# Seven block products in place of eight in the up projections of two feed-forward layers, with the modulation moved to the down projections

## The reference

```python
FFN_HIDDEN = 2816                               # 22 chunks of 128

def swiglu_ffn(x, w_in, w_down):
    h = x @ w_in                                # [512, 1024] @ [1024, 5632]
    g, u = h[..., :FFN_HIDDEN], h[..., FFN_HIDDEN:]
    return (jax.nn.silu(g) * u) @ w_down        # [512, 2816] @ [2816, 1024]

# layers 0 and 1
y = swiglu_ffn(x, ffn_w_in[i], ffn_w_down[i])
x = layer_norm(ALPHA * x + y, ln_g[i, 2], ln_b[i, 2])

# third block
c_act = jax.nn.silu(c)                                  # [1, 1024]
mod = (c_act @ mod_w[l] + mod_b[l])[:, None, :]         # [1024, 6144]: 48 blocks of 128 columns
```

## Time and profile before

| | |
|---|---|
| runs | 2298.22, 2318.23, 2323.58 us, median 2318.23 |
| profiled execution | span 2302.4 us, 47528 instructions |
| PE | busy 2235.3 us, 97% |
| DVE | busy 1271.0 us, 55% |
| ACT | busy 936.0 us, 41% |
| POOL | busy 298.9 us, 13% |
| granted clock of PE, mean | 0.994 |

### The profile page before, as it was taken

The page is one execution under the profiler, slowest core; times in us unless marked ns, Lnnn a source line. Parts: engine busy times, 40 slices in busy tenths (PEclk is TensorE's granted clock), DMA queues, the critical chain, the costliest instruction groups (busy, mean ns, idle before and its releaser), DMA issues.

```text
span 2302.4 us, 47528 instructions
## 1 busy us (share of the span) xinstructions
PE 2235.3 (97%) x18842; PEld 2140.7 (93%) x18846; DVE 1271.0 (55%) x2590; ACT 936.0 (41%) x1547; POOL 298.9 (13%) x318
## 2 busy tenths in 40 slices
PE   7999999999999999989999999999999998999998
PEld 7978999999999996978999999999989898999998
DVE  6477443665553256889463476554165655656513
ACT  4566354332222143478363252222144554444312
POOL 3000300200000052336120110000033002000001
PEclk9999999999999999999999999999999999999999
DMA  6333341255542221200252245553312202333221
GB/s 172 81 94 92 104 143 56 83 140 142 138 137 101 91 66 56 74 2 1 92 164 75 74 110 140 154 144 110 106 49 92 79 20 75 91 104 97 95 106 55
DMA packets 303947, 219.07 MB, mean 95 GB/s; under 512 B 34442, under 2 KB 290384, under 8 KB 303824
## 3 DMA queue, kind: packets, MB, share of 16 engines
q1 hardware_dynamic: 251856, 188.79, 27.4%
q10 hardware_dynamic: 50208, 25.69, 4.3%
q0 software_dynamic: 1760, 2.88, 0.4%
HBM read 207.58 MB, written 2.10 MB: 91 GB/s over the span
## 4 chain that ended last, share of the span: by engine, by line
PE 90%; ACT 4%; DVE 2%; POOL 2%; issue 1%; DMA 0%; DVEq 0%; SPq 0%; POOLq 0%; ACTq 0%
PE bank L714 69%; PE bank L831 5%; PE bank L940 4%; PE bank L910 2%; PE bank L1259 2%; PE bank L1039 1%; PE bank L1210 1%; PE bank L1108 1%; POOL ZS L2562 1%; PE bank L1100 1%; PE bank L1193 1%; ACT SQ L1559 1%; PE bank L1311 1%; ACT BI L1355 1%; POOL ZS L2531 1%
## 5 line engine op out<-in xcount | busy, mean ns | idle before, releaser
L714 PE MATMUL bank<-XH,WH 128*128 128x256 f32 (+1 forms) x3184 | 887.4, 279 | 6.2 <-DVE HF L2245 2.7
L714 PE MATMUL bank<-XH,WL 128*128 128x256 f32 (+1 forms) x3184 | 886.0, 278 | 0.0
L714 PE MATMUL bank<-XL,WH 128*128 128x256 f32 (+1 forms) x3184 | 886.0, 278 | 0.0
L681 DVE TENSOR_TENSOR WL<-RAW,WH 128x2048 fp32r<-128x2048 f32 x160 | 369.4, 2309 | 521.5 <-ACT WH L677 521.5
L714 PEld LDWEIGHTS bank<-XH,WH 128*128 128x128 f32 (+1 forms) x3184 | 599.0, 188 | 7.1 <-issue 4.1
L714 PEld LDWEIGHTS bank<-XH,WL 128*128 128x128 f32 (+1 forms) x3184 | 600.5, 189 | 0.0
L714 PEld LDWEIGHTS bank<-XL,WH 128*128 128x128 f32 (+1 forms) x3184 | 597.4, 188 | 0.2 <-issue 0.2
L677 ACT ACTIVATE WH<-RAW 128x2048 fp32r<-128x2048 f32 x171 | 327.5, 1915 | 584.1 <-PE bank L714 545.6
L714 PE MATMUL bank<-HH,WH 128*128 (+1 forms) x1056 | 293.4, 278 | 0.9 <-DVE HF L2245 0.9
L714 PE MATMUL bank<-HH,WL 128*128 (+1 forms) x1056 | 293.3, 278 | 0.0
L714 PE MATMUL bank<-HL,WH 128*128 (+1 forms) x1056 | 293.2, 278 | 0.0
(11 more groups left out here) (359 smaller groups left out, 3666.6 us busy)
## 6 DMA issues: line engine op xcount, KB each, us to landing
RAW<-in_ffn_w_in SPq DMA_DIRECT2D x88, 512.0 KB, 4.7
MB<-in_mod_w ACTq DMA_DIRECT2D x48, 512.0 KB, 5.0
RAW<-in_ffn_w_down SPq DMA_DIRECT2D x44, 512.0 KB, 4.0
RAW<-in_ffn_up SPq DMA_DIRECT2D x44, 512.0 KB, 4.6
RAW<-in_xa_w_kv SPq DMA_DIRECT2D x32, 512.0 KB, 4.4
RAW<-in_ffn_down SPq DMA_DIRECT2D x22, 512.0 KB, 3.9
RAW<-in_xa_w_q SPq DMA_DIRECT2D x16, 512.0 KB, 4.2
RAW<-in_xa_w_o SPq DMA_DIRECT2D x16, 512.0 KB, 4.0
```

The lines of the kernel that those rows point to most:

```text
L681: nc.vector.tensor_tensor(WL[:, par, :], RAW[:, par, :], f32(WH[:, par, :]), ALU.subtract).then_inc(w_split, 1)
L714: mm = nc.tensor.matmul(out_ap[:, cols], l, moving, start=(start and n == 0 and k == 0), stop=(stop and n == len(parts) - 1 and k == len(o ...
```

## The change

Units 2 to 21 of both up projections are made by Winograd's form of a two by two block product. The blocks of the tokens are x11, x12 (left 256 tokens; lower and upper half of the width) and x21, x22 (right 256 tokens), those of a weight unit are 11 and 21 (gate columns; lower and upper half of the width) and 12 and 22 (up columns). Once a layer there are four x sums: s1 = x21 + x22, s2 = s1 - x11, s3 = x11 - x21, s4 = x12 - s2. For each unit there are four weight differences: t1 = 12 - 11, t2 = 22 - t1, t3 = 22 - 12, t4 = 21 - t2. The products are p1 = x11 by 11, p2 = x12 by 21, p3 = s4 by 22, p4 = x22 by t4, p5 = s1 by t1, p6 = s2 by t2, p7 = s3 by t3, each of 4 chunks x 3 passes = 12 matmuls of 256 columns. The outputs are gate left = p1 + p2, gate right = p1 + p6 + p7 + p4, up left = p1 + p6 + p5 + p3, up right = p1 + p6 + p7 + p5. p2 adds to its own bank, and DVE adds the banks. A unit uses three banks, 4 to 6 or 0 to 2 in turn, each for more than one product in time. Line numbers from here are those of the changed kernel.

PE runs through p6(k), p1(k+1), p7(k), p2(k+1), p4(k), p5(k+1), p3(k). POOL makes the weight differences into TW (L3009), ACT the rounded parts of the gate blocks, of block 22 and of the four differences, DVE the lower parts (`gate_lo` L2543, `last_block_lo` L2550, `sum_lo` L2555). The hidden tile is kept in fp32 (HID); silu is made in halves, and the product with the up tile is `gated` (L2593). HH and HL are gone: in the down projection ACT rounds two chunks a unit into a ring RH of two places, DVE subtracts to RLO (L2616).

```diff
@@ PE
+                def product(slot, xs, to):
+                    half, cols = up_slots(f, slot)
+                    w0 = cols.start
+                    for c in range(4):
+                        wh, wl = (w[:, half, w0 + P * c:w0 + P * c + P] for w in (WH, WL))
+                        xh, xl = xs[c]
+                        for m, (a, b) in enumerate(((wh, xh), (wh, xl), (wl, xh))):
+                            mm = nc.tensor.matmul(to[:, LEFT], a, b, start=(c == 0 and m == 0),
+                                                  stop=(c == 3 and m == 2))
+                    mm.then_inc(product_done, 1)
...
+                def p4(p, k, to=None):
+                    pe.wait_ge(factor_split, factors(f, "t4", p, k))
+                    if to is None:
+                        pe.wait_ge(kept_sum, done_units(f, p, k))
+                    product(SLOT["t4"], x22, banks_of(k)[0] if to is None else to)
...
-                wide_stage(f"ffn_in{f}", xpairs(), fill, halves=True)
+                if f < 2:
+                    in_halves(f"ffn_in{f}", xpairs(), fill)
+                    up_products(f)
+                else:
+                    wide_stage(f"ffn_in{f}", xpairs(), fill, halves=True)
@@ DVE, one unit
+                def add_common(p, k):
+                    a, b, c = banks_of(k)
+                    dve.wait_ge(kept11, done_units(f, p, k))
+                    dve.wait_ge(product_done, products(f, "t2", p, k))
+                    nc.vector.tensor_tensor(E2[:, k % 2, :], E2[:, k % 2, :], a[:, LEFT], ALU.add).then_inc(kept_sum, 1)
+                    dve.wait_ge(kept_sum, done_units(f, p, k))
+                    nc.vector.tensor_tensor(UP[:, LEFT], E2[:, k % 2, :], b[:, LEFT], ALU.add).then_inc(kept12, 1)
...
+                def body(p, k, more=True):
+                    if unit_no(p, k) not in (1, 2):
+                        add12(p, k - 1, banks_of(k - 1)[1])
+                        gated(p, k - 1)
+                    sum_lo(2, p, k + 1)
+                    if unit_no(p, k) != 1:
+                        add_common(p, k)
+                        add_seventh(p, k)
+                    sum_lo(3, p, k + 1)
+                    add11(p, k + 1)
+                    if more:
+                        gate_lo(p, k + 2)
+                    if unit_no(p, k) != 1:
+                        add21(p, k, banks_of(k)[0])
+                    sum_lo(4, p, k + 1)
+                    if more:
+                        sum_lo(1, p, k + 2)
+                        last_block_lo(p, k + 2)
@@ POOL
+                def unit(p, k):
+                    r = raw_blocks(f, k)
+                    pool.wait_ge(w_loaded[(u0 + k) % 2], p * 32 + LOADED[u0 + k])
+                    for t, x, y, of in ((1, r["12"], r["11"], None), (2, r["22"], weight_sum(1), 1), (3, r["22"], r["12"], None),
+                                        (4, r["21"], weight_sum(2), 2)):
+                        if unit_no(p, k) != 2:
+                            pool.wait_ge(factor_split, factors(f, f"t{t}", p, k - 1))
+                        if of is not None:
+                            pool.wait_ge(w_sums, sums_ready(f, of, p, k))
+                        nc.gpsimd.tensor_tensor(weight_sum(t), x, y, ALU.subtract).then_inc(w_sums, 1)
```

```diff
@@ ACT
+            def mod_scale(h, par):
+
+                act.wait_ge(mod_loaded[par], h * 16 + 16)
+                for c in range(DC):
+                    ins = nc.scalar.activation(MB[:, par, c, :], MB[:, par, c, :], ACT.Copy, scale=CA[:, c:c + 1])
+                ins.then_inc(mod_scaled, 1)
...
+                mods(h0 + 9)
+                period(9, 9)
+                mods(h0 + 10)
+                mods(h0 + 11, True)
@@ DVE
+                nc.vector.tensor_reduce(ACC[:, :], MB[:, par, :, :].rearrange("p c n -> p n c"), AXX,
+                                        ALU.add).then_inc(mod_folded, 1)
...
+                with dve.Fori(0, 4) as pair:
+                    for j in range(2):
+                        mods(pair * 4 + (2 + 2 * j), pair * 4 + (2 + 2 * j), 2)
+                        period(pair * 2 + (1 + j), 1 + j)
+                mods(18, 18, 2)
+                mods(20, 20, 4)
```

More of the change, by code:

```diff
@@ L436, in build_program, with unit_no, count, products @@
         KV_CHUNKS = {3: (0, 1), 4: (2, 3), 5: (4, 5), 6: (6,), 7: (7,)}
-        MOD_S = 11
+        LEFT, RIGHT = HALF
+        WIN = FC - 2
+        PRODUCTS, FACTORS = 7 * WIN, 5 * WIN
+        MODS = [3] + [2] * 9 + [3]
+        def unit_no(p, k):
+            return 2 * p + k if isinstance(p, int) else None
+        def count(p, k, a, b):
+            return p * (2 * a) + (a * k + b)
+        def products(f, which, p, k):
+            a, b = 7, PRODUCTS * f
+            if unit_no(p, k) == 2 and which in ("11", "21", "t1"):
+                return b + {"11": 1, "21": 2, "t1": 3}[which]
+            if unit_no(p, k) == FC - 1 and which in ("t3", "t4", "22"):
+                return b + PRODUCTS + {"22": -2, "t3": -1, "t4": 0}[which]
+            return count(p, k, a, b + {"t2": -10, "t3": -8, "t4": -6, "22": -4, "11": -16, "21": -14, "t1": -12}[which])
+        def factors(f, which, p, k):
+            b = FACTORS * f
+            if unit_no(p, k) == 2 and which == "gate":
+                return b + 1
+            if unit_no(p, k) == FC - 1 and which == "t4":
+                return b + FACTORS
+            return count(p, k, 5, b + {"t2": -7, "t3": -6, "gate": -10, "t4": -4, "t1": -8}[which])
+        def sums_ready(f, t, p, k):
+            return count(p, k, 4, 4 * WIN * f + t - 8)
+        def done_units(f, p, k):
+            return count(p, k, 1, WIN * f - 1)
+        def up_slots(f, first, n=1):
+            half = (UNIT0[f"ffn_in{f}"] + first // 4) % 2
+            return half, slice(S * (first % 4), S * (first % 4) + S * n)
+        SLOT = {"11": 0, "21": 1, "t1": 2, "t2": 3, "t3": 4, "t4": 5}
+        def raw_blocks(f, k):
+            r = RAW[:, (UNIT0[f"ffn_in{f}"] + k) % 2, :].rearrange("p (c n) -> p c n", n=256)
+            return {"gate": r[:, 0:8, 0:P], "11": r[:, 0:4, 0:P], "12": r[:, 0:4, P:256], "21": r[:, 4:8, 0:P],
+                    "22": r[:, 4:8, P:256]}
+        def weight_sum(t):
+            return TW[:, t - 1, :].rearrange("p (c n) -> p c n", n=P)
+        def banks_of(k):
+            return [bank[(4, 0)[k % 2] + n] for n in range(3)]
+        SPARE = [bank[3], bank[7]]
+        def hid(p, k, cols=slice(0, S)):
+            return HID[:, bass.ds(count(p, k, 1, 0), 1), cols]
         BOFF = [0, 128, 384, 768]
@@ L2252, in unit @@
                         next_lo(dve, name, i, j)
-                    if f < DEPTH:
-                        mod_products(i + (MOD_N * f + 2), i + 2)
-                for i in range(2):
-                    unit(i, i)
-                by_pairs(dve, FC - 2, lambda i, j: unit(i + 2, j))
-                down = f"ffn_down{f}"
-                next_lo(dve, down, 0, 0)
-                with dve.Fori(0, 4) as pair:
-                    for j in range(2):
-                        next_lo(dve, down, pair * 2 + (1 + j), 1 + j)
+                down = f"ffn_down{f}"
+                if f < 2:
+                    hidden_products(f)
+                else:
+                    for i in range(2):
+                        unit(i, i)
+                    by_pairs(dve, FC - 2, lambda i, j: unit(i + 2, j))
+                    next_lo(dve, down, 0, 0)
+                    with dve.Fori(0, 4) as pair:
+                        for j in range(2):
+                            next_lo(dve, down, pair * 2 + (1 + j), 1 + j)
                 opening = UNIT0[down] + 11
```

397 lines of the change are left out of this document (344 added, 53 removed).

## The result

The changed kernel takes 2394.42 us (median of 4 runs, 2388.80 to 2406.34), the kernel before 2320.90 us (4 runs, 2298.22 to 2333.89). The ratio is 1.0346, 95% interval 1.0276 to 1.0415: slower by 3.5%. The forecast had the direction, but at 2352 us not half of the loss, and the time lies above its range. The profiled execution spans 2404.4 us against 2302.4.

A forecast was written before the change was run, and what follows sets the result against it. PE bounds the kernel before, DVE the changed up stages; -11.8 + 11.0 + 0.5 + 40.5 + 3 = +43 us gives 2346 on the profile, 2361 on the median; forecast 2352 us, range 2304 to 2385.

The forecast's parts named there:

- What bounds the kernel: Up stages: PE sets the end before; after, DVE does, at 10.8 us a unit through POOL's port, -11.8 us in both layers.
- Rival A: Up stages: the shared port does not matter, PE runs through at 84 matmuls a unit; -1 us, 2301 to 2318; chance 0.15.
- Start of the stage: Start of the up stages: PE waits 3.1 us before p1(2) and 2.4 at p6(2); +5.5 us a layer, 11.0 in both.
- Modulation in the down stage: Down stages: ACT and DVE cycle takes 11.4 us a unit with waits, PE does not wait; +0.5 us in layer 1.
- The tail: End of down stages: four modulation blocks behind the last split delay the mean; +40.5 us, the largest term, plus 3 for clock.
- Rival B: End of down stages: the tail is short, 10 us a layer, as blocks are cheap; +23 us, 2325 to 2341; chance 0.12.
- The sum: Whole kernel: -11.8 + 11.0 + 0.5 + 40.5 + 3 = +43 us on the profiled 2302.4 us, 2346.
- Rival C: Up stages: all four POOL subtractions block DVE, 12.0 us a unit; +91 us, 2395 or more; chance 0.08.
- Rival D: Up stages and tail: A and B together, -24 us, about 2285; chance 0.05.
- the seven products' 55.5 us: Up stages: 84 in place of 96 matmuls a unit save PE 28.3 and 27.2 us a layer, if it never waits.

The follow-up runs named there:

- Run 5: Changed kernel with POOL's four weight differences a unit made on only 4 of 512 columns (products then wrong): 2347.17 us, ratio 1.0200 to the kernel before.
- Run 3: Changed kernel with four places for modulation blocks in place of two, loads issued ahead of the scaling: 2334.31 us, ratio 1.0117 to the kernel before.
- run 2: Changed kernel without the last four modulation blocks of each layer, their loads and scalings included: 2352.17 us, ratio 1.0184 to the kernel before.
- run 4: Changed kernel where SP's loads wait for POOL, so DVE's last_block_lo no longer waits for POOL's fourth difference: 2369.11 us, ratio 1.0252 to the kernel before.
- run 9: Run 8 without run 4's loads, with the four weight differences a unit made by DVE instead of POOL: 2272.08 us, ratio 0.9888 to the kernel before.
- run 7: Changed kernel with five places for modulation blocks, five blocks per pair of units, none behind the last split: 2312.72 us, ratio 1.0065 to the kernel before.
- run 8: Run 7 with the fold in three additions and with run 4's loads: 2284.23 us, ratio 0.9928 to the kernel before.

## Why the prediction was wrong

**What bounds the kernel**: right. The up unit passed to DVE as forecast, at 10.88 us and 10.8, with last_block_lo and gate_lo each a microsecond over their length and PE waiting 0.74 us at p4. Run 5 takes POOL's reads away and gets PE's own unit, 9.52 us, so this is shown. Rival A falls: its 9.5 to 9.9 us come only when the collisions are gone. The terms as printed, 7.4 + 1.3 + 1.0 + 1.0, add up to 10.7 (printed as about 10.8). In sum the up stages gave -4.4 us, not -11.8: 219.6 us and not 216, of which 2.0 a layer are the wait at the first p4, counted under the start by the forecast.

**Start of the stage**: right. PE waits 3.4 us before p1 of unit 2, for 3.1 forecast, and 2.0 at that unit's p4, where the forecast had 2.4 at p6; with a wait of 0.2 between them 5.6 us a layer for 5.5 (0.7 of them recurs at p4 in every unit). In run 5, without POOL's full sums, 0.6 stays.

**Modulation in the down stage**: this is the step that failed. The forecast has "11.4 us with waits" a unit and "PE does not wait (+0.5 us in layer 1)". It had the order right, fold before load before the next block, and the block's scaling too, 2.5 us (measured 2.46, 388 ns an ACTIVATE; 0.39 was taken). But the fold with its issue was put at 1.7 us, since no row had a strided reduction and 1.21 was taken by the like of a subtraction of 1024 columns. It takes 2.0, and with transfer of the signal and issue of the load 2.5 and 2.7. That is 1.8 us more for the two, and makes 13.07 in place of 11.4, over PE's 11.3 and 10.9. In the text the upper bound of the fold, "twice that", stands; it went into the tail's bound only and not into the cycle, where 11.2 + 2 x 1.2 = 13.6 us would have shown that the unit crosses PE's. That is 32 us in two layers for 0.5. Run 3, with the same fold and the same blocks but four places and the load issued first, takes all of it away.

**The tail**: 53.9 us, in place of 40.5 and 3 for the clock. From the last split to the first read of a bank it is 19.8 us, where the steps of the forecast make 18.6, and from there to the mean 9.8 for 9.6. What was too small is ACT's lateness, forecast as 2 us in layer 0 and 5 in layer 1: the last split starts 7.2 us after PE began unit 10 in both (833.24 after 826.01, 1757.56 after 1750.35), where it was 0.3 in the kernel before, a result of the same cycle. The row sums at clock 0.50 add 2.6 us in layer 0 and 1.6 in layer 1; I had 3 for both together. Rival B, a short tail, falls: the order of the queues set it, and run 2 shows that four blocks alone are 21 to 22 us a layer.

**The sum** is then -4.4 + 6.8 + 32.2 + 53.9 = 88 us by stages. Rival C's 2395 us was met for a reason that was not C's, by luck: its units of 12 us did not come; the down stage gave 32 us more than forecast, the tail 10 and the up stage 7. (Rival D's -24 us leaves out the 3 us for the clock that A and B have; nothing hangs on it.) On the median the loss is 73.5 us. The kernel before was 18.5 us faster in its profile than in its median, the changed one 10 us slower: this is the 28 us between the two accounts. A part of it may lie in the four runs of the kernel before, whose median is 2320.90: over 24 and 17 later runs it was 2303.31 and 2301.31. The rest may be PE's pace. No run tested either.

**Where the seven products' 55.5 us went**: 28 us a layer in the collisions with POOL and in the wait for it (run 5 against the changed kernel), which is all of them. (That this is so near 55.5 is in part luck: run 5 has PE's faster pace in both layers.) Of it runs 4 and 9 give 13 and 15 us a layer back in the up stage, and run 9 also the 3.4 us before the first product. What stays between 204 and 192 is DVE's own 10.0 us a unit, against PE's 9.5, and the 3.1 us at p6 of unit 2.

What is open: what decides between 113.3 and 117.8 ns a matmul. Both stand in all kernels here, in stages of equal code (run 7: down stages of 124.6 and 120.5), and no run was made to tell.

## What to carry to other kernels

Before work is moved to an engine "with room", add up what that engine and the one that hands it data do in one period, with every wait of the one on the other in it, and take the upper bound of each unmeasured duration there: a period has an edge, and crossing it costs every unit. Two places in a hand-over between two engines make a ring when the reload stands behind the consumer in the producer's queue; two more places, with the load issued before the scaling, took 60 us off here, and work left behind the last regular step stood in the open almost in full (21 to 22 us for four blocks). Compare cycles with cycles: a stage's time divided by its units holds the start and the end as well (10.33 us in run 4, where the cycle is 10.10). Help from POOL is not free for a DVE that reads two operands in SBUF: count what a POOL instruction overlaps there as DVE time (1.0 us of 1.3 here), and try the same work on DVE.

## What the runs showed of the hardware

- A TENSOR_REDUCE of 128x1024 to 128x128 over a stride takes 1.98 us (L2481), three dependent additions of 512, 256 and 128 columns 1.47 (run 8).
- POOL subtractions of 512 columns lengthened DVE instructions with two SBUF inputs by 1.0 to 1.1 us each (2204 ns for 1225, 1661 for 693) and those with a bank as input not at all (0.41 to 0.42 us beside the POOL instruction of 647.41); moved to DVE, 0.6 us each, they took 10.02 us a unit in place of 10.10.
- An ACTIVATE of 128x128 with a scale in SBUF takes 388 ns and starts every 0.30 us, as the 396 ns of the earlier trace rows let expect: eight take 2.46 us.
- PE's granted clock was 0.50 at 861 to 868 us, after 25 us with only eight matmuls of 24 columns, and 0.50 at 836 to 841 us in run 2, after 3.3 us of the same. The row sums, 2.7 us before, took 5.3 us each time.
